# Sliding attention: weights scaled on GpSimd, outputs copied out of PSUM on VectorE

## The chip, the cores and the metric

The kernel runs on one core of a Trainium2 chip. The metric is the device time of one execution in microseconds (us), taken as the median of several runs. Engines carry the profile's short names: PE is TensorE (PEld its weight loads), DVE is VectorE, ACT is ScalarE, POOL is GpSimd, SP is SyncE.

## What is computed

The reference runs a chain of layers in float32. Four blocks come last, over 528 positions of width 1024, and the first and the last of these four are sliding-window attention (`attention_branch`). It has 16 query heads of 64 features that share 4 key/value heads, and every query sees the 128 positions up to its own. A learned sink per head joins each softmax. Cut to what matters:

```python
s = jnp.einsum('bnqhgd,bnkhd->bnhgqk', qb, kk) * (A_HD ** -0.5)
s = jnp.where(mask[None, :, None, None], s, -jnp.inf)
m = jnp.maximum(s.max(axis=-1), sink)
e = jnp.exp(s - m[..., None])
p = e / (e.sum(axis=-1) + jnp.exp(sink - m))[..., None]
o = jnp.einsum('bnhgqk,bnkhd->bnqhgd', p, vv)
...
return (o * jax.nn.silu(z.astype(jnp.float32))).astype(u.dtype) @ w_out
```

## The kernel before

Each engine has its own program, written out in order, and the programs meet only at semaphores. The function `window(i)` stands once in the program of each engine; it runs for `i` = 0 and 1, the two attention layers. Projections and rotary embedding come first; then the attention proper, which is all that the change touches, then the output projection `A0_out` or `A1_out`.

The attention is cut into 20 steps, `m` = 0 to 19. Step `m` takes query tile `m // 4` and key/value group `m % 4`, so four heads at a time. Tile 0 has 128 queries against 128 keys (steps 0 to 3), tiles 1 to 3 have 128 queries against 256 keys (steps 4 to 15), and tile 4 has 16 queries against 144 keys (steps 16 to 19). One step goes through these stages:

- **scores** (PE, L1461): products of queries and keys into one of two pairs of PX banks.
- **bias_max** (DVE, L2972 and L2977): for each of four heads, one custom instruction adds the band mask, writes the scores to `wS[m % 3]` in SBUF and leaves the smallest negated score; the row sink is added in `w_es`.
- **exps** (ACT, L2135 and L2138): exponentials in place in `wS`, with row sums.
- **normalise** (DVE, L2983, L2984 and L2987): sum plus sink, reciprocal into `w_rc`, and four multiplications of `wS` (one per head, in place) by the reciprocal.
- **turn** (PE, L1474): transposes of the weights into PL banks 0 and 1; **turned** (ACT, L2149) copies them to `wPT[m % 2]`.
- **values** (PE, L1488): products of weights and values into PL bank `2 + m % 2`; **outputs** (ACT, L2157) copies them to `Z2`.
- **gated** (POOL, L3419): the output times the opened gate `zgate`, two inputs, in place.

The order on each engine is fixed in its loop:

- PE: scores(0), scores(1), then for each `m`: scores(m+2), values(m-1), turn(m).
- DVE: bias_max(0), then for each `m`: bias_max(m+1), normalise(m). After steps 4 and 5 it also makes sums of weight tiles for the output projection (L2464, L2465, L2467 after step 4, L2470 after step 5). After the loop come 16 additions of blocks of `Z2` (L2481 to L2491), which the output projection needs for its third product on.
- ACT: exps(0), then for each `m`: exps(m+1), turned(m), outputs(m-1).
- POOL: one wait for all gates, then gated(m) for each `m`.

There are three `wS` buffers; bias_max(m+1) waits for turn(m-2) to have read its buffer. PL banks 0 and 1 are a single buffer between turn and turned. The output projection on PE (L1212) starts when all 20 gated steps are counted in `wa_out`.

Of the kernel before, what the change touches and what calls it, by code (L numbers as in the profile page):

```python
# [9 lines left out]
ALU = mybir.AluOpType  # L10
ACT = mybir.ActivationFunctionType
AX = mybir.AxisListType

P = 128
# [147 lines left out]
def build(nc, x_dram, mem_in, meta_in, w_tiles, w_narrow, w_cmp, consts, pick_halves, params, out, stop=None):  # L162
    ctx = ExitStack()
    with ctx:
# [3 lines left out]
        def sem(name):  # L168
            return ctx.enter_context(nc.semaphore(name))
# [12 lines left out]
        PL = ctx.enter_context(nc.psum_tensor("PL", [P, 4, 512], F32))  # L182
# [10 lines left out]
        def blocks(buf, T, at=0, n=None):  # L193
# [4 lines left out]
        Z1, Z2 = blocks(Z, T1, 0, 32), blocks(Z, T2, 0, 32)  # L198
# [76 lines left out]

        na_rows, na_s, na_max, na_exp, na_nrm, na_tps, na_pt, na_v, na_done = (
            sem(n) for n in ("na_rows", "na_s", "na_max", "na_exp", "na_nrm", "na_tps", "na_pt", "na_v", "na_done"))
        wa_s, wa_max, wa_exp, wa_nrm, wa_tps, wa_pt, wa_o, wa_oc, wa_out = (
            sem(n) for n in ("wa_s", "wa_max", "wa_exp", "wa_nrm", "wa_tps", "wa_pt", "wa_o", "wa_oc", "wa_out"))
        conv_done, conv_act = sem("conv_done"), sem("conv_act")  # L280


# [229 lines left out]
        def w_span(i):  # L512

            k0 = max(0, P * (i - 1))
            return min(P, T2 - P * i), k0, min(T2, P * i + P)
# [1245 lines left out]
        def _(act):  # L1761
# [323 lines left out]
            def window(i, ready):  # L2085
                n = f"A{i}"
                norm(n, ready)
                for g in range(6):
                    first_product(n + "_in", g)
                    for b in ((2 * g - 2, 2 * g - 1) if g else ()):  # L2090
                        act.wait_ge(psum_free, LIN[n + "_in"]["unit0"] + 3 + b)
                        act.activation(qk_sq[b], Z2[:, b, :], ACT.Square).then_inc(wq_sq, 1)
                act.wait_ge(wq_sum, i + 1)
                act.activation(pair(qk_rows, T2), psb(PX[0:20], w_pair("sum", 0), T2), ACT.Sqrt, scale=1.0 / 64,
                               bias=K("eps", 0, 1)[0:20]).then_inc(wq_root, 1)
                for j, (rows, turned_rows) in enumerate(SWAPS):
                    for q in range(4):
                        to = 32 * (q + 1 - 2 * (q % 2))
                        act.dma_start(turned_rows[to:to + 32], rows[32 * q:32 * q + 32]).then_inc(swap_in[j], 16)
                act.wait_ge(wq_vps, 2 * i + 1)  # L2100
                at = w_pair("v", 0)
                for x in range(2):
                    d = vdup[:, 2 * x:2 * x + 2, :, :].rearrange("p k g c -> p (k g) c")
                    src = PX[:, at + x, :].rearrange("p (n c) -> p n c", c=64)
                    ins = act.activation(d[:, :, 0:64], src, ACT.Copy)
                ins.then_inc(wq_v, 1)
                act.wait_ge(wq_vps, 2 * i + 2)
                src = PX[0:META, w_pair("v", 1), 0:256].rearrange("p (n c) -> p n c", c=64)
                act.activation(vdup[0:META, 4, :, 0:64], src, ACT.Copy).then_inc(wq_v, 1)

                def open_gate(u):
                    act.wait_ge(psum_free, LIN[n + "_z"]["unit0"] + 3 + u)
                    act.activation(zgate[:, u, :], zgate[:, u, :], ACT.Silu).then_inc(wq_z, 1)

                open_gate(0)
                act.wait_ge(wq_tps, i + 1)
                at = w_pair("rs", 0)
                act.activation(w_rs[:, 0:4, :], PX[:, at, 0:80].rearrange("p (i r) -> p i r", i=4), ACT.Copy, scale=-0.125)
                act.activation(w_rs[0:META, 4, :], PX[0:META, at, 80:100], ACT.Copy, scale=-0.125).then_inc(wq_rs, 1)
                open_gate(1)  # L2120
                open_gate(2)
                for x in range(2):
                    act.wait_ge(wq_kn, 2 * i + x + 1)
                    act.dma_start(keyp[64:128, 2 * x, 1, :], Z2[0:64, 8 + x, :]).then_inc(key_half[x], 16)
                    act.dma_start(keyp[0:64, 2 * x + 1, 0, :], Z2[64:128, 8 + x, :]).then_inc(key_half[x], 16)
                    act.activation(keyp[0:64, 2 * x, 0, :], Z2[0:64, 8 + x, :], ACT.Copy)
                    act.activation(keyp[64:128, 2 * x + 1, 1, :], Z2[64:128, 8 + x, :], ACT.Copy).then_inc(wq_kd, 1)
                for u in range(3, 8):
                    open_gate(u)

                def exps(m):
                    nq, k0, k1 = w_span(m // 4)
                    j = m % 3
                    act.wait_ge(wa_max, N_W * i + m + 1)
                    act.activation(w_es[j][0:nq], w_es[j][0:nq], ACT.Exp)  # L2135
                    for h in range(4):
                        S = wS[j][0:nq, h, 0:k1 - k0]
                        ins = act.activation(S, S, ACT.Exp, scale=-1.0, bias=w_nm[j][0:nq, h:h + 1],  # L2138
                                             accum_out=w_sm[j][0:nq, h:h + 1])
                    ins.then_inc(wa_exp, 1)  # L2140

                def turned(m):
                    nq, k0, k1 = w_span(m // 4)
                    act.wait_ge(wa_tps, N_W * i + m + 1)
                    if m >= 2:
                        act.wait_ge(wa_o, N_W * i + m - 1)
                    for c, a in enumerate(range(k0, k1, P)):
                        kn = min(P, k1 - a)
                        ins = act.activation(wPT[m % 2][0:kn, c, 0:4 * nq], PL[0:kn, c, 0:4 * nq], ACT.Copy)  # L2149
                    ins.then_inc(wa_pt, 1)  # L2150

                def outputs(m):
                    q_tile, g = m // 4, m % 4
                    nq = w_span(q_tile)[0]
                    act.wait_ge(wa_o, N_W * i + m + 1)
                    src = PL[:, 2 + m % 2, 0:2 * nq].rearrange("p (x t) -> p x t", x=2)
                    act.activation(Z2[:, 12 + 2 * g:14 + 2 * g, P * q_tile:P * q_tile + nq], src, ACT.Copy).then_inc(wa_oc, 1)  # L2157

                exps(0)
                for m in range(N_W):  # L2160
                    if m + 1 < N_W:
                        exps(m + 1)
                    turned(m)
                    if m:
                        outputs(m - 1)
                outputs(N_W - 1)
                quadrants(n + "_out")

            def mlstm(ready):
# [167 lines left out]
        def _(dve):  # L2337
# [6 lines left out]
            def step(ins):  # L2344

                counted(ins)
                dve.wait_ge(dve_step, own[0])
# [563 lines left out]
            def window(i):  # L2911
# [64 lines left out]
                    s = 16 * i + 4 * g  # L2976
                    dve.tensor_tensor(w_es[j][0:nq], w_nm[j][0:nq], Q("sinks", s, s + 4)[0:nq], ALU.add).then_inc(wa_max, 1)  # L2977

                def normalise(m):
                    nq, k0, k1 = w_span(m // 4)  # L2980
                    j = m % 3
                    dve.wait_ge(wa_exp, N_W * i + m + 1)
                    step(dve.tensor_tensor(w_sm[j][0:nq], w_sm[j][0:nq], w_es[j][0:nq], ALU.add))  # L2983
                    step(dve.reciprocal(w_rc[j][0:nq], w_sm[j][0:nq]))  # L2984
                    for h in range(4):
                        S = wS[j][0:nq, h, 0:k1 - k0]
                        ins = dve.tensor_scalar(S, S, w_rc[j][0:nq, h:h + 1], None, ALU.mult)  # L2987
                    ins.then_inc(wa_nrm, 1)

                bias_max(0)  # L2990
                for m in range(N_W):
                    if m + 1 < N_W:
                        bias_max(m + 1)
                    normalise(m)
                    if m in (4, 5):
                        weight_sums(n + "_out", 0, m - 4)
                for g in range(4):
# [408 lines left out]
        def _(pool):  # L3406
            def window(i):
                pool.wait_ge(wq_tab, i + 1)
                for r, b in enumerate(ROPED):
                    pool.wait_ge(swap_in[swap_of(b)], 64 * (i + 1))  # L3410
                    pool.tensor_tensor(Z2[:, b, :], Z2[:, b, :], cos_k if b >= 8 else cos_q, ALU.mult).then_inc(wq_cos, 1)
                pool.wait_ge(wq_z, 8 * i + 8)
                for m in range(N_W):
                    q_tile, g = m // 4, m % 4
                    nq = w_span(q_tile)[0]
                    cols = slice(P * q_tile, P * q_tile + nq)
                    pool.wait_ge(wa_oc, N_W * i + m + 1)
                    o = Z2[:, 12 + 2 * g:14 + 2 * g, cols]
                    pool.tensor_tensor(o, o, zgate[:, 2 * g:2 * g + 2, cols], ALU.mult).then_inc(wa_out, 1)  # L3419

            def head_rows_spread():

# [175 lines left out]
```

## Time and profile before

| what | value |
|---|---|
| median of 3 runs | 3611.8 us (3610.3 to 3612.57) |
| span of the profiled execution | 3607.4 us |
| PE busy | 3446.0 us, 96% of the span |
| DVE busy | 1998.2 us, 55% |
| ACT busy | 715.4 us, 20% |
| POOL busy | 88.1 us, 2% |
| chain that ended last | PE 88%, DVE 8%, issue 2%, ACT 1%, DMA 1% |

The span goes from the first to the last instruction of the one execution that was profiled. No time of its own is listed for that execution; the median of the runs shown is 4.4 us above its span. Busy shares are averages over the whole program, in which most stages are bound by PE. The chain that ended last is followed back from the last instruction through whatever released each step.

### The profile page before, as it was taken

The page shows a single profiled execution, that of the slowest core. Times are in us where ns is not written, and L with a number is a line of the kernel's source. Part 1 is how long each engine was busy: PE and PEld are TensorE (multiplying, and loading weights), DVE is VectorE, ACT ScalarE, POOL GpSimd, SP SyncE. Part 2 cuts the span into 40 slices and gives each one's busy share as a digit, 9 for nine tenths or more (in the row PEclk, how much of TensorE's full clock was granted, in tenths as well). Part 3 has the DMA queues.
Part 4 walks back from the last instruction along what each step waited for, and adds up shares of the span by engine and source line. Part 5 has one row for each costly group of instructions (what it writes and reads, how often), then busy time and mean ns, then how long its engine had stood idle before and what let it go on. Part 6 is the DMA issues. An engine that isn't in the chain of part 4 may idle for free.

```text
span 3607.4 us, 43951 instructions
## 1 busy us (share of the span) xinstructions
PE 3446.0 (96%) x16699; PEld 2722.7 (75%) x16699; DVE 1998.2 (55%) x4671; ACT 715.4 (20%) x1763; POOL 88.1 (2%) x105
## 2 busy tenths in 40 slices
PE   8987999999999999999998988999999999999988
PEld 3484788888754568888887766888887888887766
DVE  4472367554404784675544558643354656558566
ACT  2231021100013551211001135022212011121143
POOL 0000000000000000000000021000000000000110
PEclk9998999999999999999999999999999999999999
DMA  3200312222210003122222220212211222102311
GB/s 130 82 13 27 125 47 82 94 82 94 105 47 36 16 33 118 58 82 82 94 82 82 71 83 24 82 71 77 74 65 45 102 74 89 41 24 84 112 42 48
DMA packets 39975, 254.09 MB, mean 70 GB/s; under 512 B 5796, under 2 KB 5924, under 8 KB 11616
## 3 DMA queue, kind: packets, MB, share of 16 engines
q1 hardware_dynamic: 31616, 224.41, 17.6%
q0 software_dynamic: 3664, 15.07, 1.2%
q10 hardware_dynamic: 4496, 11.89, 1.2%
q8 instruction: 134, 2.20, 0.3%
q14 instruction: 65, 0.53, 0.0%
HBM read 242.68 MB, written 2.18 MB: 68 GB/s over the span
## 4 chain that ended last, share of the span: by engine, by line
PE 88%; DVE 8%; issue 2%; ACT 1%; DMA 1%; ACTq 0%; POOL 0%; POOLq 0%; DVEq 0%
PE PL L1212 26%; PE PX L1212 20%; PE PL L923 14%; PE PL L1560 4%; PE PL L1407 3%; PE PL L907 2%; PE PX L1669 2%; DVE SCR L2972 2%; PE PL L1325 1%; DVE SCR L2987 1%; PE PL L1585 1%; PE PX L1345 1%; PE PL L1712 1%; PE PL L1374 1%; PE PX L933 1%
## 5 line engine op out<-in xcount | busy, mean ns | idle before, releaser
L923 PE MATMUL PL<-xn,ring 128*128 128x264 f32 (+1 forms) x1600 | 501.6, 471 | 11.2 <-DVE xn L2366 10.7
L923 PEld LDWEIGHTS PL<-xn,ring 128*128 128x128 f32 x1600 | 304.4, 192 | 193.7 <-issue 161.8
L2409 DVE TENSOR_TENSOR Z<-PL,SCR 128x512 f32<-128x512 f32 (+3 forms) x104 | 63.9, 614 | 447.0 <-PE PL L923 349.2
L1212 PE MATMUL PL<-Z,ring 128*128 128x256 f32 (+1 forms) x1248 | 297.4, 389 | 10.4 <-DVE Z L3362 8.6
L1212 PEld LDWEIGHTS PL<-Z,ring 128*128 128x128 f32 x1248 | 241.3, 194 | 49.8 <-DVE Z L3362 9.7
L1212 PE MATMUL PL<-AUX,ring 128*128 128x256 f32 (+1 forms) x1056 | 243.9, 379 | 0.0
L1212 PEld LDWEIGHTS PL<-AUX,ring 128*128 128x128 f32 x1056 | 200.6, 190 | 27.6 <-DVE AUX L2740 0.2
L1212 PE MATMUL PL<-xn,ring 128*128 128x264 f32 (+1 forms) x864 | 204.2, 389 | 12.7 <-DVE xn L2366 11.6
L1212 PEld LDWEIGHTS PL<-xn,ring 128*128 128x128 f32 x864 | 165.8, 192 | 42.9 <-issue 12.1
L1840 ACT ACTIVATE SCR<-PL 128x256 f32<-128x256 f32 (+1 forms) x72 | 27.6, 383 | 737.2 <-PE PL L1212 737.2
L1212 PE MATMUL PX<-Z,AUX 128*128 128x264 f32 (+1 forms) x704 | 163.8, 384 | 2.7 <-DVE Z L3170 2.7
L1212 PE MATMUL PX<-AUX,ring 128*128 128x256 f32 (+1 forms) x640 | 152.5, 381 | 0.0
L1212 PEld LDWEIGHTS PX<-Z,AUX 128*128 128x128 f32 x704 | 133.7, 190 | 24.2 <-issue 3.1
L1560 PE MATMUL PL<-xn,ring 128*128 128x264 f32 x640 | 150.3, 388 | 0.0
L2556 DVE TENSOR_TENSOR SCR<-SCR,PL 128x256 f32<-128x256 f32 (+1 forms) x72 | 30.4, 422 | 213.8 <-PE PL L1212 213.8
L1212 PEld LDWEIGHTS PX<-AUX,ring 128*128 128x128 f32 x640 | 121.6, 190 | 17.8
L1560 PEld LDWEIGHTS PL<-xn,ring 128*128 128x128 f32 x640 | 119.7, 190 | 19.3
L1810 ACT ACTIVATE SCR<-resid 128x512 f32<-128x512 f32 (+1 forms) x88 | 53.8, 632 | 381.1 <-DVEq L2598 239.7
L1407 PE MATMUL PL<-xn,ring 128*128 128x264 f32 x512 | 119.6, 397 | 0.0
L1407 PEld LDWEIGHTS PL<-xn,ring 128*128 128x128 f32 x512 | 100.1, 196 | 19.1 <-issue 1.4
L1840 ACT ACTIVATE AUX<-PL 128x264 f32<-128x264 f32 x44 | 17.1, 389 | 413.4 <-PE PL L1212 413.4
L1212 PE MATMUL PL<-Z,AUX 128*128 128x264 f32 (+1 forms) x352 | 88.6, 396 | 8.1 <-DVE AUX L2470 3.4
(514 smaller groups left out, 6043.3 us busy)
## 6 DMA issues: line engine op xcount, KB each, us to landing
ring<-w_tiles SPq DMA_DIRECT2D x212, 1024.0 KB, 4.8
Z<-Z ACTq DMA_DIRECT2D x16, 264.0 KB, 5.0
SCR<-head_rows POOLq DMA_DIRECT2D x16, 264.0 KB, 3.7
AUX<-norm_scratch POOLq DMA_DIRECT2D x8, 528.0 KB, 6.6
cst<-consts ACTq DMA_DIRECT2D x1, 2188.5 KB, 15.4
resid<-x ACTq DMA_DIRECT2D x4, 512.0 KB, 9.3
Z<-norm_scratch POOLq DMA_DIRECT2D x4, 512.0 KB, 8.0
AUX<-mem POOLq DMA_DIRECT2D x2, 1024.0 KB, 5.1
```

The costliest lines, as they stand in the source:

```text
L907: mm = pe.matmul(PL[:, 2 * h + c, 0:e - a], ring[t % 2][:, k, P * h:P * h + P], src[:, KB * kc + k, a:e], start=kc == 0 and k == 0, stop=k ...
L923: mm = pe.matmul(PL[:, 2 * h + c, 0:e - a], ring[t % 2][:, k, P * h:P * h + P], src_block(name, k)[:, a:e], start=k == 0, stop=k == KB - 1)
L933: mm = pe.matmul(PX[0:G, at + c, 0:e - a], K("sum_row", 7 - b // N["per"], 7 - b // N["per"] + G), sq_buf[:, bb % 4, a:e], start=b == 0, s ...
L1212: mm = pe.matmul(ps, lhs(k), rhs(k), start=kc == 0 and k == 0, stop=kc == per - 1 and k == 3)
L1325: mm = pe.matmul(PL[:, 3, :], ring[t % 2][:, k, P * (u % 2):P * (u % 2) + P], X1[:, k, :], start=k == 0, stop=k == KB - 1)
L1407: mm = pe.matmul(PL[:, 2 * h + c, 0:e - a], ring[t % 2][:, k, P * h:P * h + P], X2[:, k, a:e], start=k == 0, stop=k == KB - 1)
L1560: mm = pe.matmul(PL[:, 2 * c, 0:HALF], ring[t % 2][:, k, P * (u % 2):P * (u % 2) + P], X2[:, k, c * HALF:(c + 1) * HALF], start=k == 0, st ...
L1669: mm = pe.matmul(ps, k, q, start=True, stop=True)
L1810: act.activation(sq, src[b], ACT.Square).then_inc(norm_sq, 1)
L1840: act.activation(quad_work(name)[2 + n % 2], quad_bank(name, "m1"), ACT.Copy).then_inc(qd_c, 1)
L2409: ins = dve.tensor_tensor(d, ps, f, ALU.mult)
L2972: ins = dve.tensor_tensor_reduce(wS[j][0:nq, h, 0:k1 - k0], K("band", b0, b0 + k1 - k0)[0:nq], src, w_rs[0:nq, q_tile, 4 * g + h:4 * g + h ...
```

## The change

On DVE, `normalise` becomes `inverse`: it ends with the reciprocal and signals the new semaphore `wa_inv`. The four multiplications go to POOL, which signals `wa_nrm`. The copies of the outputs go from ACT to DVE, two steps late: in the loop's turn `m`, DVE makes bias_max(m+1), inverse(m), outputs(m-2). POOL makes normalise(m), gated(m-2) in its turn `m`, and its wait for all gates stands before the first gated step. No DMA, no buffer and no order on PE is changed.

```diff
 (ACT)
-                def outputs(m):
-                    q_tile, g = m // 4, m % 4
-                    nq = w_span(q_tile)[0]
-                    act.wait_ge(wa_o, N_W * i + m + 1)
-                    src = PL[:, 2 + m % 2, 0:2 * nq].rearrange("p (x t) -> p x t", x=2)
-                    act.activation(Z2[:, 12 + 2 * g:14 + 2 * g, P * q_tile:P * q_tile + nq], src, ACT.Copy).then_inc(wa_oc, 1)
-
                 exps(0)
                 for m in range(N_W):
                     if m + 1 < N_W:
                         exps(m + 1)
                     turned(m)
-                    if m:
-                        outputs(m - 1)
-                outputs(N_W - 1)
 (DVE)
-                def normalise(m):
+                def inverse(m):
                     nq, k0, k1 = w_span(m // 4)
                     j = m % 3
                     dve.wait_ge(wa_exp, N_W * i + m + 1)
                     step(dve.tensor_tensor(w_sm[j][0:nq], w_sm[j][0:nq], w_es[j][0:nq], ALU.add))
-                    step(dve.reciprocal(w_rc[j][0:nq], w_sm[j][0:nq]))
-                    for h in range(4):
-                        S = wS[j][0:nq, h, 0:k1 - k0]
-                        ins = dve.tensor_scalar(S, S, w_rc[j][0:nq, h:h + 1], None, ALU.mult)
-                    ins.then_inc(wa_nrm, 1)
+                    dve.reciprocal(w_rc[j][0:nq], w_sm[j][0:nq]).then_inc(wa_inv, 1)
+
+                def outputs(m):
+                    q_tile, g = m // 4, m % 4
+                    nq = w_span(q_tile)[0]
+                    dve.wait_ge(wa_o, N_W * i + m + 1)
+                    src = PL[:, 2 + m % 2, 0:2 * nq].rearrange("p (x t) -> p x t", x=2)
+                    dve.tensor_copy(Z2[:, 12 + 2 * g:14 + 2 * g, P * q_tile:P * q_tile + nq], src).then_inc(wa_oc, 1)
 
                 bias_max(0)
-                for m in range(N_W):
+                for m in range(N_W + 2):
                     if m + 1 < N_W:
                         bias_max(m + 1)
-                    normalise(m)
+                    if m < N_W:
+                        inverse(m)
+                    if m >= 2:
+                        outputs(m - 2)
                     if m in (4, 5):
                         weight_sums(n + "_out", 0, m - 4)
 (POOL)
-                pool.wait_ge(wq_z, 8 * i + 8)
-                for m in range(N_W):
+                def normalise(m):
+                    nq, k0, k1 = w_span(m // 4)
+                    j = m % 3
+                    pool.wait_ge(wa_inv, N_W * i + m + 1)
+                    for h in range(4):
+                        S = wS[j][0:nq, h, 0:k1 - k0]
+                        ins = pool.tensor_scalar(S, S, w_rc[j][0:nq, h:h + 1], None, ALU.mult)
+                    ins.then_inc(wa_nrm, 1)
+
+                def gated(m):
                     q_tile, g = m // 4, m % 4
                     nq = w_span(q_tile)[0]
                     cols = slice(P * q_tile, P * q_tile + nq)
+                    if m == 0:
+                        pool.wait_ge(wq_z, 8 * i + 8)
                     pool.wait_ge(wa_oc, N_W * i + m + 1)
                     o = Z2[:, 12 + 2 * g:14 + 2 * g, cols]
                     pool.tensor_tensor(o, o, zgate[:, 2 * g:2 * g + 2, cols], ALU.mult).then_inc(wa_out, 1)
+
+                for m in range(N_W + 2):
+                    if m < N_W:
+                        normalise(m)
+                    if m >= 2:
+                        gated(m - 2)
```

## Rows read from the trace of the kernel before

**Rows 1.** The chain that ended last inside the first attention, shares by line.
```profile
by line: DVE SCR L2972 34.1%; DVE SCR L2987 25.7%; issue 7.2%; PE PL L1474 4.5%; DVE tiny L2984 4.0%; DVE tiny L2977 3.7%; PE PX L1461 3.4%; PE PL L1488 3.3%; PE PL L1212 2.1%; ACT SCR L2138 1.9%; DVE tiny L2983 1.9%; ACT L2135 1.6%; DVE AU
```

**Rows 2.** Windows, both attentions: length, then busy time (count) of PE, PEld, DVE, ACT, POOL, PEclk, DMA.
```profile
2141.20:2219.70 78.50, 57.56 (x450) 36.61 (x449) 74.32 (x313) 61.50 (x238) 13.58 (x20) 0.90 0.04 15
3473.70:3552.00 78.30, 55.43 (x449) 35.10 (x448) 74.78 (x313) 61.74 (x238) 13.51 (x20) 0.93 0.04 15
```

**Rows 3.** Timeline, one step with 256 keys: start, duration, engine, line, operation, count.
```profile
2176.80 0.22 ACT L2135 ACTIVATE tiny<-tiny 128x4 f32<-128x4 f32 x1
...
2178.33 0.53 DVE L2972 CUSTOM_DVE_ANT_0 SCR<-cst,PX,tiny 128x256 f32<-128x256 f32 x1
...
2178.46 1.09 PE L1474 MATMUL PL<-cst,SCR 128*128 128x128 f32 x8 [0.68 <-DVE SCR L2987]
2178.77 0.19 ACT L2138 ACTIVATION_READ_ACCUMULATOR SCR<-SCR,tiny 128x1 f32 x1
...
2179.59 1.09 ACT L2149 ACTIVATE SCR<-PL 128x512 f32<-128x512 f32 x2 [0.63 <-PE PL L1474]
...
2180.29 0.16 DVE L2977 TENSOR_TENSOR tiny<-tiny,par 128x4 f32<-128x4 f32 x1
...
2180.56 0.18 DVE L2984 RECIPROCAL tiny<-tiny 128x4 f32<-128x4 f32 x1
...
2180.73 1.08 PE L1488 MATMUL PL<-SCR,Z 128*64 128x256 f32 x8
2180.77 1.67 DVE L2987 TENSOR_SCALAR SCR<-SCR,tiny 128x256 f32<-128x256 f32 x4
...
2181.03 0.73 POOL L3419 TENSOR_TENSOR Z<-Z,AUX 128x256 f32<-128x256 f32 x1 [3.30 <-ACT Z L2157]
```

**Rows 4.** Timeline, from one turn to the next, about step 15.
```profile
2202.66 1.10 PE L1474 MATMUL PL<-cst,SCR 128*128 128x128 f32 x8 [0.68 <-DVE SCR L2987]
...
2203.79 1.09 ACT L2149 ACTIVATE SCR<-PL 128x512 f32<-128x512 f32 x2 [0.63 <-PE PL L1474]
...
2206.17 1.09 PE L1474 MATMUL PL<-cst,SCR 128*128 128x128 f32 x8
```

**Rows 5.** Timeline, a small DVE addition beside a POOL instruction.
```profile
2158.29 0.73 POOL L3419 TENSOR_TENSOR Z<-Z,AUX 128x256 f32<-128x256 f32 x1 [2.37 <-ACT Z L2157]
...
2158.47 0.56 DVE L2977 TENSOR_TENSOR tiny<-tiny,par 128x4 f32<-128x4 f32 x1
```

**Rows 6.** Groups by line and shape, POOL then DVE, whole span: busy, mean ns of one.
```profile
L3419 POOL TENSOR_TENSOR Z<-Z,AUX 128x256 f32<-128x256 f32 x32 | 23.7, 740 | 201.9 <-ACT Z L2157 201.9
...
L3419 POOL TENSOR_TENSOR Z<-Z,AUX 128x32 f32<-128x32 f32 x8 | 3.4, 427 | 12.6 <-ACT Z L2157 12.6
...
L3465 POOL MEMSET Z<- 128x3072 f32 x1 | 2.7, 2657 | 20.9 <-DVE Z L2409 20.9
...
L3467 POOL MEMSET AUX<- 128x1152 f32 x1 | 1.1, 1052 | 0.0
...
L2556 DVE TENSOR_TENSOR SCR<-SCR,PL 128x256 f32<-128x256 f32 x68 | 28.6, 421 | 205.2 <-PE PL L1212 205.2
```

**Rows 7.** The chain inside the first attention in order: multiplications of steps 0, 4, 6, 14.
```profile
2146.20 0.89 DVE SCR L2987 x4
...
2159.36 0.04 DVE SCR L2987
...
2160.50 0.60 DVE AUX L2464
...
2168.78 0.04 DVE SCR L2987
...
2200.94 0.04 DVE SCR L2987
```

**Rows 8.** Timeline, step 19's multiplications and the start of the output projection.
```profile
2215.92 0.90 DVE L2987 TENSOR_SCALAR SCR<-SCR,tiny 16x144 f32<-16x144 f32 x4
...
2219.68 6.00 PE L1212 MATMUL PL<-Z,ring 128*128 128x264 f32 x16 [0.92 <-POOL Z L3419]
```

More of the change, by code:

```diff
@@ L277, in build @@
             sem(n) for n in ("na_rows", "na_s", "na_max", "na_exp", "na_nrm", "na_tps", "na_pt", "na_v", "na_done"))
-        wa_s, wa_max, wa_exp, wa_nrm, wa_tps, wa_pt, wa_o, wa_oc, wa_out = (
-            sem(n) for n in ("wa_s", "wa_max", "wa_exp", "wa_nrm", "wa_tps", "wa_pt", "wa_o", "wa_oc", "wa_out"))
+        wa_s, wa_max, wa_exp, wa_inv, wa_nrm, wa_tps, wa_pt, wa_o, wa_oc, wa_out = (
+            sem(n) for n in ("wa_s", "wa_max", "wa_exp", "wa_inv", "wa_nrm", "wa_tps", "wa_pt", "wa_o", "wa_oc", "wa_out"))
         conv_done, conv_act = sem("conv_done"), sem("conv_act")
```

## The prediction, made before the changed kernel ran

> **What bounds the kernel now.** PE is busy almost everywhere, so I looked for the stretches where the chain that ended last leaves PE. Inside the attention it lies on DVE [rows 1]: line 2972 (biased scores and maximum) and line 2987 (the multiplications that the change moves) make 60% of it. The windows say the same of both attentions [rows 2]: about 78.4 us each, DVE busy 74.3 and 74.8, ACT 61.5, PE 57.6, POOL 13.6. Everything after an attention waits for its last gated step, so what is won in these 78 us moves the whole rest forward, twice.
>
> One step with 256 keys shows how DVE fills it [rows 3]. From the first biased score (2178.33) to the end of the reciprocal (2180.74) are 2.41 us, the four multiplications take the rest. Steps 6 to 14 make 8 periods in 2168.78 to 2200.94 [rows 7], 4.02 us each. The multiplications also pay for POOL: with the gated step inside them they take 1.67 us [rows 3], in step 4 without it 1.14 (2159.36 to 2160.50) [rows 7]. A small DVE addition of two SBUF inputs, 0.16 us elsewhere [rows 3], lasts 0.56 and ends as POOL's instruction ends [rows 5]. So the two engines exclude each other on some operations.
>
> **What a POOL multiplication costs.** No row has it; call it x for 128x256. Below: a memset only writes, and (2657 - 1052)/(3072 - 1152) = 0.836 ns a column with 0.09 us fixed gives 0.30 us [rows 6]. Above: the gated product of the same shape reads two inputs and takes 0.74 [rows 6]; nothing excludes a dearer one. One input lies between none and two, so I take the middle, 0.52. For 128 columns the ends are 0.20 and, on the line between the two gated shapes, 0.56; middle 0.38, and 0.39 for 144.
>
> The Trainium skill (GPSIMD Engine Reference, Engine selection) calls elementwise work a job for VectorE, GpSimd being about 2x slower with two inputs, but roughly at line rate with one. Line rate would be 0.30 us here (an estimate: 256 columns at that page's 1.2 GHz are 0.21, and memset's fixed 0.09); the sum by it would be 3600.0. Memset's rows agree with that rate, and no run so far shows an instruction with one input.
>
> **The change part by part, per attention.**
>
> *DVE* loses 4 multiplications a step (1.1 to 1.7 us) and gets one copy out of PSUM, about 0.42 us by the addition of that shape [rows 6]. Its step becomes 2.41 + 0.42 + 0.05 = 2.9 us, no longer the bound. One addition may wait for a gated product: the four multiplications end about 2.1 us after the reciprocal, the gated step follows until 2.9, and DVE's next w_es addition is due at 2.4 (the copy's 0.42, then 1.96 from 2178.33 to 2180.29 [rows 3]). Held back to 2.9 it makes the step 3.4, still under the next bound.
>
> *ACT* loses 20 copies. It was not the bound [rows 2], so that alone is worth nothing. The copies come two steps late on DVE; values(m) on PE needs outputs(m-2), which DVE makes right after inverse(m), before turn(m) can even start: no new stall.
>
> *POOL* gets 4x a step beside 0.74: 2.8 us of work in a period, so not full. Its wait for all gates now stands behind three sets of multiplications, which is early enough, and no DMA is queued behind it there.
>
> What binds next? First, PE and ACT hand PL banks 0 and 1 to each other: turn (1.09), turned (1.09), values (1.08) [rows 3], turn again. Where DVE's work was light this loop already ran alone: from 2202.66 to 2206.17, 3.51 us [rows 4]. No part of it is changed, so no period gets below 3.5. Second, the round trip through POOL: exps 2.16 (2176.80 to 2178.96), addition and reciprocal 0.45 (2180.29 to 2180.74), 4x, turn 1.09, turned 1.09 [rows 3], three hops of 0.05 (turn ends at 2179.55, turned starts at 2179.59), then ACT starts the exps two steps on. Two periods are 4.94 + 4x, one 2.47 + 2x: 3.51 at x = 0.52, as much as the first loop. Above that x each 0.1 us costs 0.2 a period.
>
> The sum, each against its own rows:
> - Start. The first turn waits for four multiplications: 4 x 0.38 + 0.05 in place of 0.89 [rows 7]: +0.7.
> - Steps 1 to 3: PE and the short steps stay about as they are: 0.
> - Steps 4 and 5 hold the four weight sums, 0.60 each [rows 7], with two SBUF inputs, so they and the multiplications exclude each other. Before: 2159.36 to 2168.78, 9.4 us. After: 0.4 (copy) + 3 x (0.60 + 0.52) + 2.41 = 6.1 and 0.4 + 0.60 + 0.52 + 2.41 = 3.9, less 0.2 for what overlaps: 9.8. +0.4. If they don't meet, 8.1.
> - Steps 6 to 14: 8 x 3.51 = 28.1 in place of 32.2 [rows 7]: -4.1.
> - Steps 14 to 19, 2200.94 to 2215.92 [rows 7, 8]: two periods at 3.5 as now; the three small ones lose DVE's multiplications too. Between nothing and a large step's 0.5 each I take half: -0.8.
> - End. Step 19's multiplications, 4 x 0.39 + 0.05 in place of 0.90 [rows 8]: +0.7. Turn, turned, values, copy and gated follow as before.
> - The 16 additions of the output projection now start behind the last copy instead of before it. They are costed at nothing: PE's first 16 matmuls, 6.00 us [rows 8], cover them: at 0.42 [rows 6] they take 6.7, begin 0.5 us earlier (a last gated product, 0.43 [rows 6], and its hops), and the last two are not needed by the third product. Without that cover PE would stand for up to 6 us.
>
> Together -3.1 us an attention, -6.2 for both. The profiled span, 3607.4, lies 4.4 under the median of the runs; I take the difference over to the median: 3611.8 - 6.2 = **3605.6**.
>
> **Rivals.**
>
> *One input is nearly free*, x between memset's 0.30 and 0.45, say 0.36 (0.25 for 128 columns). The loops are bound by PE and ACT at 3.5 all the same, only the edges shrink: +0.2, -0.1, -4.1, -1.2, +0.2, so -5.0 an attention, **3601.8**. At 0.30 itself they vanish and the three small steps gain 0.5 each: -5.9, 3600.0. For it: memset's low price. Against it: an input must be read.
>
> *POOL is the slow way* (the other side). At x = 0.74 the round trip is 2.47 + 1.48 = 3.95, hardly under the 4.02 of now: steps 6 to 14 give -0.6, start +1.4, sums +1.5, steps 14 to 19 +0.9, end +1.4: +4.6, both 9.2, **3621.0**. Between -6.2 at 0.52 and +9.2 at 0.74 the sum turns positive at about x = 0.61 and passes 0.2% at 0.71. For it: the gated products, the only arithmetic on POOL that the trace has, cost that. Against it: they read two inputs.
>
> *The exclusion comes back on the other side.* The multiplications leave DVE, but the additions of w_es and of the sums stay, and now POOL is busy much of each step. If both wait for a whole POOL instruction in each step, DVE's step is 2.9 + 2 x 0.52 = 3.9: -1.0 in steps 6 to 14, +0.6 after them, the rest as above: +1.4, both 2.8, **3614.6**. For it: the 0.56 us row [rows 5]. Against it: at the forecast's period the multiplications end before the additions are due. The Trainium skill (SBUF — State Buffer, SBUF: two separate sides) has the port pair as an exclusive lock for the whole instruction, against VectorE work in a 2-port mode or with two SBUF inputs; the trace agrees with the 0.56 us.
>
> That the change does not do what it says is not open: the instructions move as written.
>
> **How the numbers follow.** A measurement can tell about 0.2%, 7.2 us, from no change, so faster means under 3604.6 and slower over 3619.0. The forecast (x between 0.45 and 0.61) has 0.42, of which 0.16 lies below 3604.6. The nearly free input has 0.26, all of it faster. Exclusion has 0.17, all of it the same. POOL dear has 0.15, slower. That gives 0.42 faster, 0.43 the same, 0.15 slower. The range goes from under the memset's bound (3600) to just short of the 0.74 case: 3599 to 3619; what it leaves out is a POOL as dear as its two-input product, or dearer.
>
> **What the changed profile would show.** Right: POOL multiplications of 0.45 to 0.6 us; the chain inside the attention no longer on line 2972 but alternating between turn, turned and values at 3.5 us a period; no 0.9 us multiplications; ACT's wait for turn as the longest there; an attention of about 75.3 us. Wrong: a mean above 0.61 with turn waiting for POOL in each step; or small DVE additions of 0.5 us and more in each step; or an output projection whose third product waits for the additions.

## The result, and the profile after

| | before | after |
|---|---|---|
| median of 4 runs on one chip | 3611.05 us (3609.26 to 3612.57) | 3635.62 us (3632.43 to 3643.41) |
| ratio to before, 95% interval | | 1.0071 [1.0057, 1.0084] |
| span of the profiled execution | 3607.4 us | 3641.6 us |
| POOL busy | 88.1 us | 213.8 us |
| first turn to the start of the output projection, both attentions | 72.56 and 72.45 us | 84.92 and 85.11 us |

The change makes the kernel slower by 24.6 us; the prediction had 3605.6 and a range that ended at 3619. The profiled execution of after is the slowest of its four, so its 34.2 us of longer span overstate the median's loss. Of these 34.2, the two attentions hold 25.0 by the last line of the table (12.36 and 12.66), and some 1.5 more stand ahead of each first turn. The other 6.2 lie in stretches that the change does not touch, 4.9 of them between the two attentions; their cause is not shown.

The same two windows as [rows 2], now 15 us longer each, columns PE, PEld, DVE, ACT, POOL, PEclk, DMA:

```profile
2141.20:2234.90 93.70, 64.18 (x455) 41.16 (x453) 54.83 (x247) 56.62 (x218) 76.29 (x100) 0.83 0.03 12
3493.00:3586.30 93.30, 63.10 (x452) 40.27 (x450) 54.51 (x247) 56.62 (x218) 76.29 (x100) 0.85 0.04 12
```

DVE gave up 20 us of its 74 and POOL took up 63. POOL is now the engine with most work, and PE's granted clock has fallen from 0.90 and 0.93 to 0.83 and 0.85. The reason for the 63 is in the groups of POOL by line and shape (busy, mean ns of one):

```profile
L3414 POOL TENSOR_SCALAR SCR<-SCR,tiny 128x256 f32<-128x256 f32 x96 | 90.0, 956 | 10.4 <-DVE tiny L2974 10.4
...
L3425 POOL TENSOR_TENSOR Z<-Z,AUX 128x256 f32<-128x256 f32 x32 | 23.4, 731 | 0.0
L3414 POOL TENSOR_SCALAR SCR<-SCR,tiny 16x144 f32<-16x144 f32 x32 | 20.0, 634 | 1.1 <-DVE tiny L2974 1.1
L3414 POOL TENSOR_SCALAR SCR<-SCR,tiny 128x128 f32<-128x128 f32 x32 | 18.7, 600 | 100.7 <-DVE tiny L2974 100.7
```

A multiplication with one tensor and a column of factors takes 0.956 us, more than the gated product with two full inputs (0.731). On DVE the same work took 0.42 [rows 3: 1.67 for four]. The chain inside the first attention, which [rows 1] gave to DVE, shows it:

```profile
by line: POOL SCR L3414 39.0%; PE PL L1474 12.6%; PE PX L1461 11.7%; DVE SCR L2962 11.5%; PE PL L1212 5.3%; ACT SCR L2138 3.2%; POOL Z L3425 2.7%; issue 2.5%; PE PL L1488 1.9%; PE PL L1407 1.8%; DVE tiny L2967 1.6%; DVE tiny L2974 1.5%; ACT
...
2182.55 3.65 POOL SCR L3414 x4
2186.24 1.79 PE PL L1474 x8
2188.04 2.02 PE PX L1461 x8
2190.08 0.54 DVE SCR L2962
...
2192.60 3.65 POOL SCR L3414 x4
...
2202.49 3.66 POOL SCR L3414 x4
2206.19 1.09 PE PL L1474 x8
2207.29 1.09 PE PX L1461 x8
...
2210.38 0.78 DVE tiny L2967
...
2211.54 3.63 POOL SCR L3414 x4
```

This is a ring of two steps. The reciprocal releases four multiplications (3.65), they release the turn, **scores of a later step stand behind the turn in PE's order**, and the biased scores made from them stand ahead of the next reciprocal but one in DVE's order. It takes 10.05 us (2182.55 to 2192.60) where turn and scores take 1.79 and 2.02, and 9.05 (2202.49 to 2211.54) where they take 1.09 each. The difference comes from TensorE's clock: turn and scores take 1.63 us more at the lower clock, and 0.62 of it is won back at the small addition (L2967), which waits for POOL in the second ring only (0.78 us instead of 0.16). Windows of PE's wait, the turn behind it and the scores, same columns:

```profile
2174.50:2176.15 1.65, 0.00 (x0) 0.00 (x0) 1.58 (x8) 0.87 (x4) 1.65 (x3) 1.00 0.00 0
2176.15:2178.10 1.95, 1.90 (x9) 1.58 (x10) 0.15 (x1) 0.00 (x0) 1.95 (x3) 0.52 0.00 0
2178.10:2180.00 1.90, 1.90 (x11) 1.27 (x12) 0.00 (x0) 1.80 (x6) 1.90 (x3) 0.59 0.00 0
```

PE did nothing for 1.65 us, waiting for POOL, and the turn and most of the scores after it ran near the lower level of 1.2 GHz (granted clock 0.52 and 0.59). By stretches of the first attention, from the starts of the turns:

| stretch | before | after | forecast difference | measured |
|---|---|---|---|---|
| multiplications ahead of the first turn | 0.89 | 2.36 | +0.7 | +1.5 |
| turn of step 0 to step 4 | 13.43 | 16.34 | 0 | +2.9 |
| 4 to 6, the weight sums | 10.05 | 9.83 | +0.4 | -0.2 |
| 6 to 14 | 32.06 | 39.02 | -4.1 | +7.0 |
| 14 to 19, with the forecast's "end" | 14.21 | 17.09 | -0.1 | +2.9 |
| 19 to the output projection | 2.81 | 2.64 | 0 | -0.2 |

### The profile page after: what moved, and what is told of

It reads as the page before. It is cut to its first block, busy times and chain, and to the rows that moved or that the text cites. A ratio compares the mean times of both kernels' runs of the same rounds, so it can differ in the third digit from the quotient of the medians.

```text
span 3641.6 us, 43951 instructions
## 1 busy us (share of the span) xinstructions
PE 3463.1 (95%) x16699; PEld 2734.8 (75%) x16699; DVE 1962.0 (54%) x4551; ACT 705.7 (19%) x1723; POOL 213.8 (6%) x265
## 4 chain that ended last, share of the span: by engine, by line
PE 88%; DVE 6%; POOL 2%; issue 1%; ACT 1%; DMA 1%; ACTq 0%; POOLq 0%; DVEq 0%
PE PL L1212 26%; PE PX L1212 20%; PE PL L923 13%; PE PL L1560 4%; PE PL L1407 3%; PE PL L907 2%; POOL SCR L3414 2%; PE PX L1669 2%; PE PL L1325 1%; PE PL L1585 1%; PE PX L1345 1%; PE PL L1712 1%; PE PL L1374 1%; PE PX L933 1%; PE PL L983 1%
## 5 line engine op out<-in xcount | busy, mean ns | idle before, releaser
L1212 PEld LDWEIGHTS PL<-xn,ring 128*128 128x128 f32 x864 | 165.8, 192 | 42.4 <-issue 11.8
L3414 POOL TENSOR_SCALAR SCR<-SCR,tiny 128x256 f32<-128x256 f32 (+2 forms) x160 | 128.7, 820 | 112.2 <-DVE tiny L2974 112.2
```

The costliest lines, as they stand in the source:

```text
L1212: mm = pe.matmul(ps, lhs(k), rhs(k), start=kc == 0 and k == 0, stop=kc == per - 1 and k == 3)
L3414: ins = pool.tensor_scalar(S, S, w_rc[j][0:nq, h:h + 1], None, ALU.mult)
```

## The experiments

Theory after the result: the price of POOL's multiplication is the loss. Rivals: the copies on DVE hurt; PE's order makes the ring; the price is contention with DVE. The diffs are against after, except for the one that starts from before.

### The two halves of the change

Multiplications on POOL, copies back on ACT:

```diff
 (ACT)
                     turned(m)
+                    if m:
+                        outputs(m - 1)
+                outputs(N_W - 1)
 (DVE)
                     inverse(m)
-                    if m >= 2:
-                        outputs(m - 2)
```

> The copies go back to ACT, the multiplications stay on POOL. Theory (POOL's multiplication costs 0.91 us of itself, and the round trip through POOL sets the period): as slow as the changed kernel, 3630 to 3640 us, with the multiplications at 0.9 to 0.96 us. Rival (the copies, late and on DVE, are what costs): back to about 3611 us.

Measured: 3641.97 us, ratio 1.0092 [1.0075, 1.0109], 2 us over the expected range; multiplications 941 ns; 4.65 us a period in steps 6 to 14. The multiplications alone bring the whole loss. With the copies on DVE as well, after is 6 us lower (3635.62), but the two ratios differ by only 0.0021, no more than their intervals leave open, so a gain by the copies is not shown. The chain has the copy in its way on ACT, between turned (L2149) and exps (L2138):

```profile
2183.34 3.63 POOL SCR L3421 x4
...
2187.01 1.11 PE PL L1474 x8
...
2188.64 0.59 ACT SCR L2149
2189.23 0.28 ACT Z L2157
...
2189.59 1.95 ACT SCR L2138 x8
...
2192.63 3.63 POOL SCR L3421 x4
```

Copies on DVE, multiplications back on DVE:

```diff
-                    dve.reciprocal(w_rc[j][0:nq], w_sm[j][0:nq]).then_inc(wa_inv, 1)
+                    step(dve.reciprocal(w_rc[j][0:nq], w_sm[j][0:nq]))
+                    for h in range(4):
+                        S = wS[j][0:nq, h, 0:k1 - k0]
+                        ins = dve.tensor_scalar(S, S, w_rc[j][0:nq, h:h + 1], None, ALU.mult)
+                    ins.then_inc(wa_nrm, 1)
 (POOL)
-                    if m < N_W:
-                        normalise(m)
```

> The multiplications go back to DVE, the copies stay on DVE. Theory: DVE pays 0.42 us for the copy and wins about 0.5 us where the gated product no longer falls among its multiplications, so 3606 to 3616 us, near the kernel before. Rival (the late copies cost the time): near 3636 us.

Measured: 3607.16 us, ratio 0.9989 [0.998, 0.9999]; 3.84 us a period (2170.44 to 2201.13, eight steps). Two groups of DVE:

```profile
L2977 DVE TENSOR_SCALAR SCR<-SCR,tiny 128x256 f32<-128x256 f32 x96 | 27.4, 349 | 0.9
L2985 DVE COPY Z<-PL 128x256 f32<-128x256 f32 x32 | 13.3, 415 | 0.0
```

DVE gets 0.415 us of copy into each step, and still the step is shorter: the multiplications take 349 ns where they took 451 before, because the gated product now runs beside the biased scores (from 2178.47, during L2962) and not among the multiplications. The copies are the harmless half.

### PE's order

```diff
+                scores(2)
                 for m in range(N_W + 1):
-                    if m + 2 < N_W:
-                        scores(m + 2)
+                    if m + 3 < N_W:
+                        scores(m + 3)
```

> The changed kernel with PE's scores one turn earlier in its order, so that they no longer stand behind the turn that waits for POOL. Theory: the period of a large step falls from 5.0 us to POOL's own work, 4 x 0.91 + 0.74 = 4.4, about 7 us less in each attention, 3618 to 3625 us in all. Rival (POOL and DVE hold each other up, and this sets the period): 3632 to 3643 us as before the edit.

Measured: 3627.95 us, ratio 1.0044 [1.0028, 1.0061], 7.7 us below after; POOL's price stays at 938 ns. The expected 3618 to 3625 was missed. The chain no longer has scores in it:

```profile
2181.15 3.64 POOL SCR L3415 x4
...
2184.83 1.11 PE PL L1474 x8
...
2186.46 0.59 ACT SCR L2150
...
2187.14 1.97 ACT SCR L2139 x8
...
2189.13 0.68 DVE tiny L2974
...
2189.83 0.19 DVE tiny L2975
...
2190.11 3.64 POOL SCR L3415 x4
```

It is the round trip that the prediction had, turn, turned, exps, reciprocal, multiplications: 8.96 us for two steps. By the prediction's 4.94 + 4x with x = 0.91 it would be 8.58; the addition of the sink (L2974 here) takes 0.68 instead of 0.15, held back beside POOL, which covers the rest. POOL itself is all but full: the multiplications and the gated products of two steps are 2 x (3.64 + 0.73) = 8.74 us. Windows of after's ring at the full clock, then of this one, columns as above:

```profile
2202.49:2211.54 9.05, 6.02 (x49) 3.63 (x47) 6.25 (x25) 5.90 (x22) 8.65 (x11) 1.00 0.00 1
2181.15:2190.11 8.96, 6.48 (x50) 4.06 (x48) 6.01 (x25) 6.27 (x22) 8.63 (x11) 1.00 0.00 0
```

At full clock the ring through PE's order (9.05) is hardly longer than this one, so the order by itself is worth little while POOL has this much to do. That the rest of the 7.7 us is the lower clock is likely, but not shown: it is seen in one turn of each attention here (1.66 and 1.52 us, step 4) and in four in after's, with one profile of each kernel.

### The price of one multiplication

Is it the column of factors? A constant in its place (the weights are then not normalised); a single execution:

```diff
-                        ins = pool.tensor_scalar(S, S, w_rc[j][0:nq, h:h + 1], None, ALU.mult)
+                        ins = pool.tensor_scalar(S, S, 0.5, None, ALU.mult)
```

> The changed kernel with POOL's multiplications by the constant 0.5 in place of the column of reciprocals (so the weights are not normalised). Theory (a per-partition operand is what makes the form dear): 128x256 falls from 0.94 to about 0.5 us and the time below 3612 us. Rival (the form itself, one input and one scalar, is dear): 0.9 us and 3630 to 3643 us.

Is it the form? The same column as a second input that repeats it:

```diff
-                        ins = pool.tensor_scalar(S, S, w_rc[j][0:nq, h:h + 1], None, ALU.mult)
+                        ins = pool.tensor_tensor(S, S, w_rc[j][0:nq, h:h + 1].broadcast_to([nq, k1 - k0]), ALU.mult)
```

> Four two-input POOL products a step, one per head, with the reciprocal broadcast, in place of four multiplications by a column. From the one product's two shapes (1.04 us for 512 columns, 1.89 for 1024) 1.67 ns a column and 0.19 fixed: 0.61 each, 2.5 a step. Theory (the form decides, the number of instructions only adds 0.19 each): period 3.6, 3603 to 3608 us. Rival (it was the fourfold dispatch): 0.9 each and 3630 us or more.

And one product for all four heads:

```diff
-                    for h in range(4):
-                        S = wS[j][0:nq, h, 0:k1 - k0]
-                        ins = pool.tensor_scalar(S, S, w_rc[j][0:nq, h:h + 1], None, ALU.mult)
-                    ins.then_inc(wa_nrm, 1)
+                    S = wS[j][0:nq, :, 0:k1 - k0]
+                    by = w_rc[j][0:nq].rearrange("p (h a) -> p h a", a=1).broadcast_to([nq, 4, k1 - k0])
+                    pool.tensor_tensor(S, S, by, ALU.mult).then_inc(wa_nrm, 1)
```

> The four POOL multiplications by a column become one POOL product of two inputs over the four heads, the reciprocals broadcast. Theory (the price of the instruction's form decides): at the gated product's 2.1 to 2.8 ns a column 1024 columns take 2.2 to 2.9 us in place of 3.63, the period 3.6 to 3.9 us, in all 3605 to 3615 us. Rival (any multiplication on POOL costs about 3.6 us for these columns): 3630 to 3640 us.

The groups of POOL in the three kernels, the constant first:

```profile
L3414 POOL TENSOR_SCALAR SCR<-SCR 128x256 f32<-128x256 f32 x96 | 78.9, 848 | 9.3 <-DVE tiny L2974 9.3
...
L3414 POOL TENSOR_SCALAR SCR<-SCR 128x128 f32<-128x128 f32 x32 | 16.0, 523 | 101.1 <-DVE tiny L2974 101.1
```

Four products:

```profile
L3414 POOL TENSOR_TENSOR SCR<-SCR,tiny 128x256 f32<-128x256 f32 x96 | 59.4, 649 | 16.0 <-DVE tiny L2974 16.0
...
L3414 POOL TENSOR_TENSOR SCR<-SCR,tiny 128x128 f32<-128x128 f32 x32 | 11.8, 398 | 101.7 <-DVE tiny L2974 101.7
```

One product:

```profile
L3414 POOL TENSOR_TENSOR SCR<-SCR,tiny 128x1024 f32<-128x1024 f32 x24 | 45.4, 1893 | 27.8 <-DVE tiny L2974 27.8
...
L3414 POOL TENSOR_TENSOR SCR<-SCR,tiny 128x512 f32<-128x512 f32 x8 | 8.3, 1040 | 103.3 <-DVE tiny L2974 103.3
```

The constant takes 848 ns, 0.11 less than the column, so the theory that the column makes it dear fell; that one execution took 3621.52 us, between the two ranges expected. The form is dear: 2.8 ns a column with the column of factors ((956 - 600)/128), 2.5 with the constant, 2.0 as a product, 1.7 in the product of four heads ((1893 - 1040)/512), with 0.19 us fixed. The prediction had a product with two inputs above the form with one, and it lies below. The number of instructions is not the price: four products take 649 ns each, not the rival's 0.9 us. Contention with DVE is not the price either: in after, four multiplications took 3.64 us from 2176.80, while DVE stood still from 2176.3 to 2180.03.

The times follow: four products 3605.99 us, ratio 0.9988 [0.9978, 0.9998], as expected; one product 3600.64 us, ratio 0.997 [0.9958, 0.9981], with 3.35 us a period, better than the expected 3605 to 3615. One change of form on POOL turns +0.7% into -0.3%.

What is left when the multiplications cost almost nothing? Eight columns of each head instead of all (the others stay unnormalised):

```diff
-                        S = wS[j][0:nq, h, 0:k1 - k0]
+                        S = wS[j][0:nq, h, 0:8]
```

> POOL multiplies only 8 columns of each head (the rest of the weights stays unnormalised), so its price goes to the fixed part, 0.24 us by the two shapes 0.600 and 0.956. Theory (POOL's price sets the whole loss): period 3.3 to 3.5 us, bound by PE and ACT, 3594 to 3601 us in all. Rival (crossing to POOL and back, or the copies on DVE, costs by itself): 3605 us or more.

Measured: 3586.92 us, ratio 0.9941 [0.9925, 0.9957], better than expected. Timeline of one period:

```profile
2180.91 1.10 PE L1474 MATMUL PL<-cst,SCR 128*128 128x128 f32 x8
...
2182.05 1.08 ACT L2149 ACTIVATE SCR<-PL 128x512 f32<-128x512 f32 x2 [0.15 <-PE PL L1474]
...
2182.40 1.15 POOL L3414 TENSOR_SCALAR SCR<-SCR,tiny 128x8 f32<-128x8 f32 x4 [1.44 <-DVE tiny L2974]
...
2183.18 1.08 PE L1488 MATMUL PL<-SCR,Z 128*64 128x256 f32 x8
...
2184.20 0.99 PE L1474 MATMUL PL<-cst,SCR 128*128 128x128 f32 x7
```

Turn, turned, values and turn again follow one another without a gap, 3.29 us a period. That is the loop of PE and ACT which the prediction took for 3.51.

### The weight sums

The one product loses time in steps 4 to 6: its turns start at 2160.14, 2166.73 and 2172.36, 6.6 and 5.6 us apart, and 3.35 after that. The timeline there:

```profile
2158.19 1.89 POOL L3414 TENSOR_TENSOR SCR<-SCR,tiny 128x1024 f32<-128x1024 f32 x1 [0.90 <-DVE tiny L2974]
...
2158.34 2.29 DVE L2454 TENSOR_TENSOR AUX<-ring 128x512 f32<-128x512 f32 x1
...
2160.04 1.18 POOL L3424 TENSOR_TENSOR Z<-Z,AUX 128x256 f32<-128x256 f32 x1
...
2160.55 1.22 DVE L2455 TENSOR_TENSOR ring<-ring 128x512 f32<-128x512 f32 x1
```

A sum of two SBUF tensors on DVE takes 2.29 us beside the product, and the gated product 1.18 beside a sum. So the sums are placed where DVE waits, before the last copy of the gates' blocks:

```diff
                 for u in range(3, 8):
+                    if u == 7:
+                        weight_sums(n + "_out", 0, 0)
+                        weight_sums(n + "_out", 0, 1)
                     copy_out(n + "_z", u)
...
-                    if m in (4, 5):
-                        weight_sums(n + "_out", 0, m - 4)
```

First a run without this edit: the one product, the sums where they were, but PE's early scores:

> The one product, with PE's scores one turn earlier as well. Theory: at a period of 3.35 us ACT's own 3.3 is the bound, and the order costs at most 1 us an attention: 3598 to 3601 us. Rival (scores behind the turn still bind, since DVE idles 0.5 to 1.1 us before them): 3 us an attention or more, 3590 to 3595 us.

Measured: 3602.47 us, ratio 0.9982 [0.9973, 0.9991], above both ranges and no better than the one product alone. Its turns stand even further apart in step 5 (2162.97 and 2171.22). PE's order is not what holds it.

The one product with the sums moved:

> The one product, with the four weight sums of the output projection moved out of steps 4 and 5 to DVE's idle time before its last copy of a gate block, where POOL is idle too. Theory (in these two steps the sums and POOL's product exclude each other: a sum of 0.69 us lasts 2.29 there): the two steps fall from 12.2 to 6.7 us, 5 us an attention, 3588 to 3593 us in all. Rival (the sums only fill time in which DVE waits anyway): 3598 to 3602 us, as with the one product alone.

Measured: **3586.81 us, ratio 0.9937 [0.9924, 0.9951]**, just under the expected range and the best kernel of the study that computes everything; 62.11 and 61.36 us from first turn to output projection. Timeline, first the sums in DVE's wait, then two turns and a product from the steps of 3.35 us:

```profile
2136.99 0.71 DVE L2399 TENSOR_TENSOR AUX<-PL,SCR 128x528 f32<-128x528 f32 x1 [6.41 <-PE PL L1407]
2137.62 0.68 DVE L2454 TENSOR_TENSOR AUX<-ring 128x512 f32<-128x512 f32 x1
...
2166.36 1.10 PE L1474 MATMUL PL<-cst,SCR 128*128 128x128 f32 x8
...
2167.82 1.89 POOL L3415 TENSOR_TENSOR SCR<-SCR,tiny 128x1024 f32<-128x1024 f32 x1 [1.15 <-DVE tiny L2977]
...
2169.77 1.09 PE L1474 MATMUL PL<-cst,SCR 128*128 128x128 f32 x8
```

Is that the place of the sums alone? The kernel before with the sums moved:

> The kernel before with the weight sums moved in the same way; nothing else changed. Theory: with DVE the bound they cost their own 4 x 0.60 us there, without any exclusion worth naming: 2.4 us an attention, 3605 to 3608 us. Rival (the gap before the last gate block is no free time, so the start of the attention moves back by as much): 3609 to 3613 us.

Measured: 3607.68 us, ratio 0.9998 [0.9989, 1.0007]. Its profile has 70.85 and 70.98 us where before had 72.56 and 72.45, but of such a gain the time shows nothing; inconclusive. After with the sums moved:

> The changed kernel with the weight sums moved in the same way. Theory (POOL's column multiplications set the period of 5 us, in which DVE waits 2 to 4 us for scores): the sums lie in that wait, so moving them gives at most 2 us in all, 3630 to 3637 us. Rival (the exclusion in these two steps is a large part of the loss): 3622 to 3627 us.

Measured: 3632.2 us, ratio 1.007 [1.0054, 1.0085], nothing that the time can tell from after (1.0071). The sums lay in DVE's waits there, as expected. In the first attention of its profile all turns of steps 4 to 14 ran at 1.09 us, and steps 6 to 14 took 36.1 us (2168.29 to 2204.35), 4.51 a period, where after's profiled execution had 39.0. So about 3 us an attention of that execution are the clock. How often the other executions of after had it stays open, as no profile of them exists; their mean granted clocks go with their times (0.972 for the profiled one, 0.974 at 3638.66 and 0.975 at 3632.59 and 3632.43).

## Why the prediction was wrong

**The step that failed** is the price of a POOL multiplication: "One input lies between none and two, so I take the middle, 0.52". It measured 0.956 (0.600 for 128 columns, 0.634 for 144), beyond the gated product that stood as the upper end. The text had said that "nothing excludes a dearer one", but the range was cut short of it: it ended at 3619, under the 3621.0 of the rival that had been given 0.15. Most of the loss follows from this one term: the prediction's own sums, -6.2 at 0.52 and +9.2 at 0.74, continued in a line to the 0.91 that one of four takes, give 9.2 + 0.17 x 70 = +21; the median moved by +24.6. (The prediction's other sums come out as written, but for the weight sums, which give 9.9 and not 9.8.) The one product and the few columns, which lower the price and leave the rest of the change, bring the gain that was forecast and more. The Trainium skill (GPSIMD Engine Reference, Engine selection) has one input at roughly line rate, 0.30 us by the prediction's estimate; the measured 0.956 contradicts it here, and decides.

**Where the line is only roughly right.** That it comes so near is in part luck, as it misses at the other end: for a price of 0.30 the prediction has 3600.0, 11.8 us won, and the eight columns, at 0.29, won 22.5 over the kernel before of their own round. From first turn to output projection that is 61.60 us in each attention, 11 less than before; 3.2 of these come from the stretch of steps 4 to 6 (6.81 us instead of 10.05), where the sum had next to nothing, and 5.8 from steps 6 to 14, where it had 4.1.

With x = 0.91 the prediction's round trip gives 2.47 + 1.82 = 4.29 us. POOL's own work is then already more, 4 x 0.91 + 0.73 = 4.37 us a period, where the prediction had 2.8, "so not full". At full clock 4.51 was measured, at the lower clock 5.0. Three more things bear on it.
- The ring through PE's order was not in the list of what binds next: "no order on PE is changed" was true, but POOL's delay is passed on by it to the scores behind the turn.
- The exclusion did come to the other side, as the third rival said, though with one small addition in two steps, 0.68 to 0.78 us instead of 0.16, and not with two whole instructions in each. "At the forecast's period the multiplications end before the additions are due" held no longer once POOL was busy almost all the time.
- In after's profile the turns of steps 4, 6, 8 and 10 ran wholly or in part at the lower clock, each behind a wait of PE for POOL (1.74 to 2.36 us in the first attention). Such a wait alone does not explain it: turn 12 ran at 1.09 us behind 1.86, and step 4 of the multiplications alone ran at 1.09 behind 3.30 in one attention and at 1.97 behind 2.94 in the other. What else it takes stays open.

Steps 0 to 4, costed at nothing, lost 2.9 us. The chain goes there through turn and scores as well, and it ends in step 4's four multiplications, 4.57 us instead of 3.64 beside DVE's weight sums. So the +0.4 forecast for the sums came one stretch earlier, at about 0.9. Most of the rest is the price again, as step 4's multiplications had taken 1.14 us on DVE:

```profile
2161.75 4.57 POOL SCR L3414 x4
2166.37 1.97 PE PL L1474 x8
```

This is the chain of after in the first attention once more, step 4's multiplications and its turn.

**The floor of 3.5** was misread from [rows 4]: it was said to run "alone", but the eight columns showed 3.29. The turn there had still waited for DVE's multiplications, which ended at 2206.11, after PE's values (2206.01). The forecast's gain was therefore bounded too low: two kernels, the few columns and the one product with the sums moved, ran at 3587, under the range's end at 3599.

**What held.** DVE bound the steps before (the copies alone: 4.02 to 3.84 once the multiplications are free of the gated product). The copies cost DVE 0.4 us, and after's chain in the first attention has none of them before the last step. The 16 additions of the output projection stay covered: it starts 2.64 us after turn 19, the additions end at 2240.43, and its third product starts at 2243.41 without a wait. The rival "POOL is the slow way" was the right one, at 0.15; a mean above 0.71 was met, though its own price (0.74) and time (3621.0) were too low as well. The Trainium skill's lock between the engines (SBUF — State Buffer, SBUF: two separate sides) agrees with the 2.29 us of a sum that takes 0.68 alone.

## What to carry to other kernels

An operation that moves to another engine is priced by a row of that very form on that engine, and without one the range has to reach beyond the nearest form, since fewer inputs need not be cheaper. At the dear end the engine's whole load is added up again: here POOL was full. Look for the form before giving up the move: here the product for four heads at once made of a loss of 0.7% a gain, and clearing the other engine's two-input work out of its way doubled it. A delay on the new engine is followed through every in-order queue behind it.

## What was not expected of the hardware

On POOL a multiplication with one tensor and a column of factors (956 ns for 128x256) is dearer than a product of two tensors (731), and a product whose second input repeats the column is the cheapest (649, and 1893 for 128x1024). Eight columns still took 0.29 us each (1.15 for four). In after, PE's turn of step 6 took 1.97 us instead of 1.09 behind a wait for POOL of 1.74, with a granted clock of 0.52; yet with the multiplications alone on POOL a turn kept 1.09 behind a wait of 3.30.
